# Weights and activations at other offsets in on-chip memory: the high halves 32 words further, the moving tiles 32 words nearer

## The reference

```
proj = rmsnorm(x) @ w_in                      # 1024 x 9472
h = x + (g1*(ssd @ W1) + g2*(mla @ W2) + g3*(gdn @ W3)) @ w_out
x = h + square(relu(rmsnorm(h) @ w_up)) @ w_down        # 2 layers
...
x = x + g * mixer(modulate(rms_norm(x)))                # 2 layers
x = x + g * ((silu(a) * u) @ w_out), a, u = split(modulate(rms_norm(x)) @ w_in)
```

## Time and profile before

| | |
|---|---|
| median of three runs | 2430.05 us |
| profiled execution | 2421.43 us |
| its span, first to last instruction | 2419.6 us |
| mean granted TensorE clock | 0.99 |
| PE busy | 2355.6 us, 97% |
| PE weight loads busy | 2180.4 us, 90% |
| DVE, ACT, POOL busy | 1437.0, 1249.1, 280.8 us |
| read from device memory | 375.8 MB, 156 GB/s over the span |

### The profile page before, as it was taken

The page is one execution under the profiler, slowest core; times in us unless marked ns, Lnnn a source line. Parts: engine busy times, 40 slices in busy tenths (PEclk is TensorE's granted clock), DMA queues, the critical chain, the costliest instruction groups (busy, mean ns, idle before and its releaser), DMA issues.

```text
span 2419.6 us, 48140 instructions
## 1 busy us (share of the span) xinstructions
PE 2355.6 (97%) x21314; PEld 2180.4 (90%) x21314; DVE 1437.0 (59%) x2147; ACT 1249.1 (52%) x1845; POOL 280.8 (12%) x163
## 2 busy tenths in 40 slices
PE   8989999999999999999999999999999999998999
PEld 8979899999999899999998886887789998787999
DVE  6773776665477467766664347643335553676554
ACT  6746556554476465466543467532223453454543
POOL 4203000000131300001010014200000001331000
PEclk9999999999999999999999999999999999999999
DMA  6344355555535344455553245323225542223454
GB/s 222 140 158 160 140 189 185 182 193 193 198 140 183 133 157 148 169 195 189 189 192 105 105 159 191 133 111 140 105 88 191 209 159 89 91 87 140 176 194 171
DMA packets 56129, 381.00 MB, mean 157 GB/s; under 512 B 6257, under 2 KB 9841, under 8 KB 10737
## 3 DMA queue, kind: packets, MB, share of 16 engines
q1 hardware_dynamic: 55024, 374.59, 43.2%
q10 hardware_dynamic: 896, 3.33, 0.4%
HBM read 375.80 MB, written 1.05 MB: 156 GB/s over the span
## 4 chain that ended last, share of the span: by engine, by line
PE 80%; DVE 10%; ACT 7%; issue 2%; POOL 0%; DMA 0%; SPq 0%; DVEq 0%; ACTq 0%; POOLq 0%
PE ps L955 21%; PE ps L957 21%; PE ps L956 21%; DVE r L2261 3%; ACT r L1592 2%; PE ps L1036 1%; PE ps L1037 1%; PE ps L1038 1%; PE ps L914 1%; PE ps L1094 1%; PE ps L876 1%; PE ps L993 1%; PE ps L995 1%; PE ps L994 1%; PE ps L1463 1%
## 5 line engine op out<-in xcount | busy, mean ns | idle before, releaser
L955 PE MATMUL ps<-r,r 128*128 128x256 f32 (+1 forms) x4448 | 1317.1, 296 | 11.0 <-DVE r L2261 2.8
L957 PE MATMUL ps<-r,r 128*128 128x256 f32 (+1 forms) x4448 | 1301.9, 293 | 0.6 <-issue 0.6
L956 PE MATMUL ps<-r,r 128*128 128x256 f32 (+1 forms) x4448 | 1302.2, 293 | 0.0
L2261 DVE TENSOR_TENSOR r<-ring,r 128x1024 fp32r<-128x1024 f32 (+1 forms) x562 | 685.8, 1251 | 429.9 <-ACT r L1592 428.4
L955 PEld LDWEIGHTS ps<-r,r 128*128 128x128 f32 x4448 | 840.2, 189 | 49.4 <-issue 11.3
L956 PEld LDWEIGHTS ps<-r,r 128*128 128x128 f32 x4448 | 839.9, 189 | 24.5 <-issue 0.8
L957 PEld LDWEIGHTS ps<-r,r 128*128 128x128 f32 x4448 | 839.4, 189 | 24.5
L1592 ACT ACTIVATE r<-ring 128x1024 fp32r<-128x1024 f32 (+1 forms) x610 | 613.7, 1041 | 158.6 <-PE ps L957 139.1
L3209 POOL TENSOR_TENSOR slab<-slab 128x512 f32<-128x512 f32 (+1 forms) x20 | 28.6, 1432 | 1203.9 <-ACT slab L1708 1184.6
L3162 POOL TENSOR_TENSOR r<-ring,r 128x1024 fp32r<-128x1024 f32 x48 | 114.0, 2399 | 233.2 <-ACT r L1592 233.1
L2347 DVE SCALAR_TENSOR_TENSOR slab<-ps,v,slab 128x255 f32<-128x255 f32 (+1 forms) x168 | 67.8, 474 | 61.8 <-ACT slab L1660 61.8
(11 more groups left out here) (357 smaller groups left out, 2561.2 us busy)
## 6 DMA issues: line engine op xcount, KB each, us to landing
ring<-in_win SPq DMA_DIRECT2D x73, 1024.0 KB, 4.8
ring<-in_ada SPq DMA_DIRECT2D x48, 1024.0 KB, 4.8
ring<-in_fi SPq DMA_DIRECT2D x44, 1024.0 KB, 4.8
ring<-in_fo SPq DMA_DIRECT2D x36, 1024.0 KB, 4.7
ring<-in_wup SPq DMA_DIRECT2D x32, 1024.0 KB, 4.7
ring<-in_wdn SPq DMA_DIRECT2D x32, 1024.0 KB, 4.7
ring<-in_hin SPq DMA_DIRECT2D x20, 1024.0 KB, 4.8
ring<-in_nqkv SPq DMA_DIRECT2D x12, 1024.0 KB, 4.7
```

What stands on the lines that cost most here:

```text
L955: self.mm(o, hi[:, k - k0, cs], xh, k == 0, False)
L956: self.mm(o, hi[:, k - k0, cs], xl, False, False)
L957: i = self.mm(o, lo[:, k - k0, cs], xh, False, k == last)
L2261: self.tt(K.low(p), K.raw(p), K.high(p).bitcast(F32), ALU.subtract).then_inc(*self.up("w_lo_v", p))
```

## The change

The slab's tiles begin at 48 words instead of 80. The ring tensor is 64 words longer, and the places of the high weights begin 32 words further behind the four raw units. The raw units and the low parts, which are the same words, stay where they were. What follows the ring moves by 64 words.

```
-SHIFT = 80
+SHIFT = 48
+APART = 32
...
-        self.ring = self.sb("ring", [128, (2 * RAW + HI) * SLOT])
+        self.ring = self.sb("ring", [128, (2 * RAW + HI) * SLOT + 2 * APART])
         self.lows = [self.rounded(ARENA + 2 * i * SLOT, 2 * SLOT) for i in range(RAW)]
-        self.highs = [self.rounded(ARENA + 2 * (RAW + i) * SLOT, 2 * SLOT) for i in range(HI // 2)]
+        self.highs = [self.rounded(ARENA + 2 * (RAW + i) * SLOT + APART, 2 * SLOT) for i in range(HI // 2)]
```

## The result

The changed kernel takes 2409.03 us (median of five runs, 2407.09 to 2411.77) against 2427.91 us for the kernel before (five runs, 2420.52 to 2431.57): a ratio of 0.9927, 95% interval 0.9907 to 0.9947. It is faster by 18.9 us, where 8 us slower was forecast. In the next session 28 runs of the kernel before had a median of 2418.87 us (2411.74 to 2432.68), and two versions with the change's distances had ratios of 0.9947 (0.9925 to 0.9969) and 0.9960 (0.9942 to 0.9979) to them. So the gain is 0.4 to 0.7%, by the set of runs of the kernel before that it is held against; the changed distances themselves gave 2409.03, 2409.46 and 2409.59 us.

The account below looks back on a forecast made before the run. The prediction took the number of PE's matmuls times their spacing as the bound. Terms +10.4 and -2.4 summed to +8 us: 2429.4 from the profiled 2421.4, or 2438 on the median 2430.05; range 2400 to 2462.

Parts of the forecast that it names:

- The two levels: 256-column triples on line 957: whole stretches at 339.8 ns (quick) or 353.4 ns (slow) a triple, at the same clock.
- the first term: Quick 256-column triples: 2300, each losing 4.5 ns for the one load moving from distance 48 to 16, +10.4 us.
- the 0 for slow triples: Slow 256-column triples: 1890 taken as unchanged, 0 us, with bounds from -25.7 us to 0.
- the slow level goes: Rival: the odd load breaks the slow rhythm and all 256-column triples become quick, -28 us, 2402; chance 0.22.
- The prediction's own last sentence: Sign on line 957: whole stretches staying at 340 or 353 ns, only shares changing, would make the 4.5 ns term false.
- The 512-column term: 544 triples 512 columns wide: each gains 4.4 ns, a third of 13 ns, -2.4 us (bounds -7.2 and 0).
- Lines 1036 to 1038: 256 triples with x stationary: two loads keep distance 16, one gets 48; taken as 0, bounds 0 and -3.5 us.
- Float32 matmuls: Plain float32 matmuls between slab and cst, line 876: distances swap between 48 and 16; 0, at most 0.7 us.
- DVE and ACT: Weight preparation, lines 2261 and 1592: any longer DVE work, at 20 ns each 11 us, hidden by PE; 0.
- They follow PE ... and add no term: Buffers freed by PE set ACT's and SP's pace; these follow PE in either direction, adding 0.
- the rival with 109.1 ns for all three matmuls: 256-column triples reach line 876's spacing at all three loads, gaining 77 us, 2353; 109.1 ns rival's chance 0.06.
- The rule that loading weights takes nothing from the running matmul: Skill rule on TensorE's independent read ports: sum 0, 2430 us; the rival that nothing moves had chance 0.17.

Follow-up runs that it names:

- e6: Changed kernel with the low half of each x tile 32 words further, so loads and moving tiles both jump: 2474.58 us, ratio 1.0218.
- e4: Changed kernel with the high weights another 64 words further (96 instead of 32): 2409.59 us, ratio 0.9960.
- e3: Changed kernel with everything 32 words further, all distances kept: 2409.46 us, ratio 0.9947.
- e1: Tiles' half of the change alone: against the changed kernel, high weights not moved, all three loads at distance 16: 2437.97 us, ratio 1.0065.
- e2: Weights' half of the change alone: against the changed kernel, tiles back at 80, loads at distances 16, 48, 16: 2433.08 us, ratio 1.0049.
- e12: Changed kernel with the tiles 8 words nearer (40 instead of 48), loads at distances 40, 8, 40: 2449.90 us, ratio 1.0126.

## Why the prediction was wrong

**What bounds the kernel** was right. The time follows the spacing of the triples, from 340 ns at 2409 us to 362.8 ns at 2475, while DVE, ACT and transfers did the same work: start to start the 3811 triples took 1321.1 us in the changed kernel's profile and 1395.4 in e6's, 74 us more, and the span is 68 us longer.

**The two levels, and that d modulo 64 could matter** were right, and are now shown: e4 for the period, e3 that a common shift doesn't matter, e1 with a whole stretch moved from quick to slow and line 1038 from slow to quick by nothing but the distance of the tiles from everything else.

**The step that failed is the first term**, "I take a third of 13.6, 4.5 ns, for the one load of three that moves", +10.4 us, together with the 0 for slow triples. It took the price of a load at d = 16 from line 1037, where all loads are at 16 and all triples slow, and divided it by three. The price is not a sum over loads. e1 shows that with three loads at 16 nine triples in ten are slow, and e2 that two are worse than none; yet one, the right one, costs nothing and takes nearly all of the slow level away: in the changed kernel the window at 1130 us went from 353.4 to 341.9 ns. The quick triples were to lose 10.4 us and kept their 340 ns; the slow ones were to stay and gave back about 16 us (1180 triples less on the slow level at 13.6 ns each), within their bound of -25.7. That was the rival "the slow level goes", at 0.22 and 2402 us. The prediction's own last sentence named the sign by which its term would be false, levels of whole stretches with other shares, and that is what happened. Its argument that d = 16 is on the slow level held for nine triples in ten when all loads are there, and was of no use for a mixture. That the measured time lies inside the range of 2400 to 2462 us owes nothing to the sum: the range had been drawn wide enough for a full exchange of levels either way.

**How many were slow**: 45% was taken, 34% counted in this execution (1280 of 3811); the mean duration of 278.4 ns, from which the 45% came, is raised by starts after gaps. It also varies: 42 runs of the kernel before (28, 7 and 7) lie between 2410.13 and 2432.68 us, those of the changed kernel between 2407.09 and 2411.77. 22.6 us of spread would be some 1660 triples on either level, an estimate from 13.6 ns each. No second profile of the kernel before was taken, so that its spread is this share is argued, not shown.

**The 512-column term**: -2.4 us forecast; 544 x 5.3 ns = -2.9 measured. The size agrees, but not as a third of each triple: in the changed kernel 169 of the 512 that another follows directly took 685 to 692 ns, 154 took 693 to 697, and 160 stayed at 698 to 704. With all loads at 16 (e1) 472 of the 512 took 685 to 692.

**Lines 1036 to 1038** were costed at 0 and kept 353.5 ns. **Float32 matmuls**: 0; line 877 keeps a mean of 291 ns. **DVE and ACT**: 0; medians 1224 and 1047 as before.

**"They follow PE ... and add no term"** was off by 8 us. Of 22.3 us that the matmuls gave up, 14.3 arrived: PE's idle time went from 64.0 to 72.0. 4.1 us of it stand before line 956, 3.5 of them for the low weights of line 2262, and 1.7 before line 994. The waits for line 2262 rose from 7 to 13, and 9 of the 13 lie between 110 and 280 us and between 700 and 910 us. There a quicker PE overtakes the preparation of its weights and waits longer. The chain agrees: DVE's share of it rose from 10 to 14%, ACT's from 7 to 9%.

One slip changes nothing: by its own spacings the rival with 109.1 ns for all three matmuls would gain 78 us, not 77.

**The rule that loading weights takes nothing from the running matmul** (the Trainium skill, "TensorE: Matmul & The Clock Gate", section "Step-by-step: what each phase is for") was given 0.17 as a rival, with 2430 us. Twelve kernels with the same instructions and other distances, from 2409 to 2475 us, disagree with it as a rule on time: the places of the moving and the loaded operand, one against the other, cost up to 22.8 ns a triple, and nearly as much with no other engine active. The estimate of 109.2 ns for 256 columns, worked out from N/2.4 + 2.5 ns in the same page's section "Wait — 56ns, not 53.3ns?", was reached by no triple here; the shortest level is 113.3 ns a matmul.

**What stays open** is the mechanism: why a jump of 32 words between loads can end the slow level and the same jump between moving operands did not, and why only with the low load at 16. The traces show when instructions start, not when their reads fall on each other.

## What to carry to other kernels

Where back-to-back matmuls of one form run at two spacings at the same clock, look at the places of the two operands modulo 64 words before looking at the schedule; one or two constants in a memory map were worth from -0.7 to +1.6% here, and +2.2% with the low halves of x moved as well. Measure combinations, not halves: each half of this change alone was slower than before, and no cost for one load could be added up. And take a level's price from rows with the same pattern, since here a load's distance had no price of its own apart from those of the other loads.

## What the runs showed of the hardware that was not expected

- Places count modulo 64 words (256 bytes a partition): 64 more words between high and low weights left 340.1 ns a triple (e4), 8 words at the tiles made it 353.3 (e12).
- With all three loads at one distance, d = 48 and d = 16 both have a quick (340 ns) and a slow (353) level, held for whole stretches; at 48 2399 of 3811 triples were quick, at 16 343. d = 32 has no quick level (360.1 ns in the stretch read).
- For 512 columns d = 16 for all loads is better than 48 (686 ns against 700), for 256 columns 48.
- The worst of the twelve placements, both operands jumping by half a period (e6), costs 22.8 ns a triple of 340, 6.7%, in a pattern that repeats after five triples.
- The slow levels stand with DVE, ACT, GpSimd and the DMAs all idle: 353 ns in 46 such triples of the kernel before, 362.3 in 126 of e6.
